# ScalarE's two steps of an attention round in the other order: exponentials of the present unit first, then the copy of the turned probabilities of three rounds back

## The reference

```python
def first_block(x, mem, ...):            # two layers
    h = rmsnorm(x, g_mix[l])
    dq, dk, dv, c_q, c_kv_kr, xq, gate_logits = jnp.split(h @ w_in[l], split_idx, axis=-1)
    y_diff = diff_attention(...) @ w_diff_o[l]      # 8 heads, two causal softmax maps each, keys of 64
    y_mla = latent_attention(...) @ w_mla_o[l]      # 8 heads, causal, keys of 96, values of 64
    y_mem = memory_cross_attention(...) @ w_cross_o[l]   # 4 heads of 128 over 256 memory rows
    gates = jax.nn.sigmoid(gate_logits + b_gate[l])
    x = x + (gates[0] * y_diff + gates[1] * y_mla + gates[2] * y_mem) @ w_out[l]
    x = x + jnp.square(jax.nn.relu(rmsnorm(x, g_mlp[l]) @ w_mlp1[l])) @ w_mlp2[l]

def hybrid_layer(x, ...):                # the second block, two layers
    p = split_cols(rmsnorm_2(x, norm_w) @ w_in)
    o_a = dsa_mixer(...)        # scores pick the keys, then a softmax over them
    o_b = nsa_mixer(...)        # three softmaxes: compressed, selected, window
    o_c, o_d = shortconv_mixer(...), pool_mixer(...)
    return x + jnp.concatenate([silu(gate) * o ...], axis=-1) @ w_out
```

## Time and profile before

| | us |
|---|---|
| median of 3 runs | 2902.8 (2900.97 to 2902.9) |
| the profiled execution | 2904.73 |
| its span | 2902.3 |
| TensorE matmuls busy | 2706.6 (93%) |
| TensorE weight loads busy | 2196.5 (76%) |
| GpSimd busy | 1868.5 (64%) |
| VectorE busy | 1076.0 (37%) |
| ScalarE busy | 758.2 (26%) |
| exponentials (L619), 352 | 172.5 busy |
| copies (L631), 176 | 116.6 busy |
| maxima (L605), 176 | 132.6 busy |
| transpositions (L546), 784 | 126.2 busy |

### The profile page before, as it was taken

The page is one execution under the profiler, slowest core; times in us unless marked ns, Lnnn a source line. Parts: engine busy times, 40 slices in busy tenths (PEclk is TensorE's granted clock), DMA queues, the critical chain, the costliest instruction groups (busy, mean ns, idle before and its releaser), DMA issues. The chain is left out here.

```text
span 2902.3 us, 38743 instructions
## 1 busy us (share of the span) xinstructions
PE 2706.6 (93%) x14204; PEld 2196.5 (76%) x14204; DVE 1076.0 (37%) x1936; ACT 758.2 (26%) x1469; POOL 1868.5 (64%) x1562
## 2 busy tenths in 40 slices
PE   6999999999999997999999999999998998989987
PEld 5788776877888886788777778888887875677755
DVE  4452555211210113344374310310112487526783
ACT  3331564100120201341465100120111214212251
POOL 5647223888898995748420888898886772366704
PEclk9999999999999998999999999999998997989988
DMA  4323101333233233323100233223234320142202
GB/s 122 102 56 83 33 8 27 87 94 92 91 98 95 94 98 77 113 66 82 46 8 9 82 92 98 88 95 98 95 97 84 89 79 28 33 86 76 80 1 73
DMA packets 159284, 214.77 MB, mean 74 GB/s; under 512 B 51696, under 2 KB 69360, under 8 KB 159088
## 3 DMA queue, kind: packets, MB, share of 16 engines
q1 hardware_dynamic: 120336, 207.27, 24.3%
q10 hardware_dynamic: 38752, 4.95, 1.4%
HBM read 210.06 MB, written 2.10 MB: 73 GB/s over the span
## 5 line engine op out<-in xcount | busy, mean ns | idle before, releaser
L293 POOL TENSOR_TENSOR weight_parts<-weight_ring,zero 128x512 fp32r<-128x512 f32 (+3 forms) x736 | 790.2, 1074 | 735.5 <-PE ps L376 368.4
L296 POOL TENSOR_TENSOR weight_parts<-weight_ring,weight_parts 128x512 fp32r<-128x512 f32 (+4 forms) x804 | 1062.6, 1322 | 129.4 <-ACT weight_parts L304 71.0
L378 PE MATMUL ps<-h_feature_major_high,weight_parts 128*128 128x512 f32 x2304 | 589.4, 395 | 17.9 <-POOL weight_parts L293 11.6
L378 PEld LDWEIGHTS ps<-h_feature_major_high,weight_parts 128*128 128x128 f32 x2304 | 431.3, 189 | 124.4 <-POOL weight_parts L293 19.4
L376 PE MATMUL ps<-weight_parts,h_feature_major_high 128*128 128x512 f32 (+3 forms) x1920 | 438.4, 368 | 18.7 <-POOL weight_parts L293 7.8
L376 PEld LDWEIGHTS ps<-weight_parts,h_feature_major_high 128*128 128x128 f32 x1920 | 341.7, 192 | 71.3 <-POOL weight_parts L293 8.2
L378 PE MATMUL ps<-h_feature_major_low,weight_parts 128*128 128x512 f32 x1152 | 311.5, 393 | 0.0
L376 PE MATMUL ps<-weight_parts,ut_high 128*128 128x512 f32 x1024 | 254.7, 390 | 0.0
L378 PEld LDWEIGHTS ps<-h_feature_major_low,weight_parts 128*128 128x128 f32 x1152 | 218.5, 190 | 46.5
L376 PE MATMUL ps<-weight_parts,h_feature_major_low 128*128 128x512 f32 (+3 forms) x960 | 231.6, 364 | 0.0
L524 PE MATMUL ps<-arena 64*128 64x512 f32 (+9 forms) x704 | 179.4, 509 | 49.6 <-ACT probs L619 29.4
(11 more groups left out here) (255 smaller groups left out, 2912.9 us busy)
## 6 DMA issues: line engine op xcount, KB each, us to landing
weight_ring<-in_w_in SPq DMA_DIRECT2D x272, 256.0 KB, 2.6
weight_ring<-in_w_mlp SPq DMA_DIRECT2D x256, 256.0 KB, 2.7
weight_ring<-in_w_out SPq DMA_DIRECT2D x64, 256.0 KB, 2.5
weight_ring<-in_w_mem_kv SPq DMA_DIRECT2D x32, 256.0 KB, 2.7
weight_ring<-in_w_diff_o SPq DMA_DIRECT2D x32, 256.0 KB, 2.7
weight_ring<-in_w_in SPq DMA_DIRECT2D x32, 170.0 KB, 2.4
weight_ring<-in_w_in SPq DMA_DIRECT2D x32, 168.0 KB, 2.2
weight_ring<-in_w_in SPq DMA_DIRECT2D x32, 163.0 KB, 2.2
```

The costliest lines, as they stand in the source:

```text
L293: self.nc.gpsimd.tensor_tensor(high, raw, self.m["zero"][:].broadcast_to([P, raw.shape[1]]), ALU.add).then_inc(self.s["slab_high"], 1)
L296: self.nc.gpsimd.tensor_tensor(low, raw, high.bitcast(F32), ALU.subtract).then_inc(self.s["slab_split"], 1)
L378: last = self.nc.tensor.matmul(banks[:, t, :], w[:, cut], h, **ends)
```

## The change

In the four calls of `A.steps` on ScalarE, `(0, A.exp)` comes ahead of `(3, A.copy)` in the list. TensorE, VectorE, GpSimd, SyncE and all waits keep their order and their form.

```diff
--- before.py
+++ after.py
@@ -1013,7 +1013,7 @@
             full(act, "dk1")
             square("dk1")
             empty("dk1", qk[:, :, 3 * W512:])
-            A.steps(0, U1, (3, A.copy), (0, A.exp), ahead=2)
+            A.steps(0, U1, (0, A.exp), (3, A.copy), ahead=2)
             roots(st_d[:, :, 24:32])
             empty("lat0", latq[:, :, 0:LATW // 2], width=LATW // 2)
             full(act, "lat1")
@@ -1042,7 +1042,7 @@
                     a.activation(km[:, t, 4 * k:4 * k + 4, 0:MNOPE], bank[:, :, 0:MNOPE], ACT.Copy, scale=st_lat[:, t, 1:2])
                     last = a.activation(vm[:, t, 4 * k:4 * k + 4, :], bank[:, :, MNOPE:], ACT.Copy, scale=st_lat[:, t, 1:2])
                 last.then_inc(emptied, 1)
-            A.steps(U1, U2, (3, A.copy), (0, A.exp), between={prep_rounds[-2]: lambda: roots(st_both)})
+            A.steps(U1, U2, (0, A.exp), (3, A.copy), between={prep_rounds[-2]: lambda: roots(st_both)})
             for k in range(2):
                 scaled(f"m_t{k}", [(qmt[0:MQK, 4 * k + h, :], h, MQK, SEQ, mqg[0:MQK]) for h in range(4)])
             for k in range(2):
@@ -1052,7 +1052,7 @@
                     act.wait_ge(s["weighted"], u + 1)
                     a.activation(ot[0][:, 8 + units[u]["pair"], :], ps[:, units[u]["bank"], :], ACT.Copy).then_inc(s["high_written"], 1)
 
-            A.steps(U2, U3, (3, A.copy), (0, A.exp), (4, round_high))
+            A.steps(U2, U3, (0, A.exp), (3, A.copy), (4, round_high))
             roots(st_o)
             for name in merge_order:
                 if name[0] == "o":
@@ -1583,7 +1583,7 @@
             empty("f1", [(fm[:, 8:10, :], L.banks("f1")[:, 0:2, :], ACT.Copy, 1.0), (fm[:, 10:12, :], L.banks("f1")[:, 2:4, :], ACT.Silu, 1.0)])
             empty("f2", [(fm[:, 12:14, :], L.banks("f2")[:, 0:2, :], ACT.Copy, 1.0), (fm[:, 14:16, :], L.banks("f2")[:, 2:4, :], ACT.Silu, 1.0)])
             empty("cmp_t", [(kcmpt, L.banks("cmp_t")[:, 0, 0:NCMP], ACT.Copy, 1.0)])
-            A.steps(0, U, (3, A.copy), (0, A.exp))
+            A.steps(0, U, (0, A.exp), (3, A.copy))
             L.square_right(act, 1, junk)
 
         @block.vector
```

## The result

The changed kernel takes 2983.28 us (median of 4 runs, 2979.08 to 2986.27) against 2901.89 us (4 runs, 2900.78 to 2902.9): a ratio of 1.0283, interval [1.027, 1.0296]. It is slower, as forecast; the forecast was 2969 us, the range 2925 to 3008. The profiled spans are 2902.3 and 2984.4 us, +82.1. In the experiments three executions that took 5368 to 9296 us (two of the kernel before, one of the kernel with the copy between the exponentials) are left out of every median, ratio and interval.

What follows compares the result with a forecast made beforehand. TensorE was taken to bound latent attention, VectorE's turn to decide in differential attention's start and the second block. First block 44, second 12, clock 10: +66 us on 2904.7, less 1.9, gives 2969; range 2925 to 3008.

Steps and rivals of the forecast that it cites:

- The mechanism: Attention rounds: TensorE's turning T(j+1) waits for ScalarE's copy C(j), now behind exponentials E(j+3); exponentials gain at most one copy, 0.38 to 0.81 us.
- The latent halves: Latent attention lap: turning of 512 keys to that of 384 takes 6.78 us (5.92 before), then 5.65 (4.63 before).
- The late differential halves: Differential attention's last twelve rounds, no woven work: 6.11 us (5.69 before) and 5.42 (4.82 before); +3 us a layer.
- Rounds 3 to 20 with woven work: Differential attention: the chain through VectorE's division and woven piece takes 7.87 us against 5.76; +11 us a layer, bounds 6 and 17.
- The second block: At 12 waits of scores for exponentials, a quarter of 1.6 to 2.7 us is lost; +6 us a layer, bounds 0 and 12.
- Latent attention: A lap of 10.55 us gets 1.9 longer over 3.3 laps, +6.3; with the last closing round +6.5 us a layer.
- Late differential rounds and cross attention: Last twelve differential rounds: three laps of +1.0, +3 us a layer; cross attention: six rounds, +1.5 us a layer.
- The clock: TensorE's waits bring seven more spells at the lower clock, about 1.4 us each over all layers: +10, bounds 0 and 24.
- (a): Rival, chance 0.04: wherever scores wait for exponentials, these come one copy earlier, 44 waits times 0.6 = 26 us, 2877.
- (b): Rival, chance 0.04: exponentials and copy both come soon enough, as TensorE has weighting and scores between; no change, 2903.
- (c): Rival, chance 0.14: VectorE's woven work hides the chain's loss; only stretches without it lose, 22 us, 2925.
- (d): Rival, chance 0.18: the attention passes see some 30 spells at 1.2 GHz instead of seven, +42 in place of +10, 3001.

## Why the prediction was right, and where its sizes were off

**The mechanism** held as it was put: C(j) behind E(j+3), T(j+1) behind C(j), a closed chain over two rounds. The latent halves were forecast at 6.78 and 5.65 us and measured at 6.84 and 5.72. The late differential halves are these turnings, of 512, 384 and 512 keys, after:

```profile
405.56 0.85 PEld L546 LDWEIGHTS ps<-ident,probs 128*128 128x128 f32 x8 [0.35 <-ACT probs L619]
...
411.73 0.64 PEld L546 LDWEIGHTS ps<-ident,probs 128*128 128x128 f32 x6
...
417.21 0.85 PEld L546 LDWEIGHTS ps<-ident,probs 128*128 128x128 f32 x8 [0.25 <-issue]
```

6.17 and 5.48 us, forecast 6.11 and 5.42. In the two latent ones the copy's signal took 0.11 and 0.12 us, where 0.05 was assumed. Shown by experiment: in cross attention the alternating banks take the link T(j+1) on C(j) away, and with it the whole loss ahead of the last maximum; the copy between the exponentials about halves the loss of the four passes together. Two of the signs that were to show it came out weaker than written: the copies' waits for turnings fell to 42.9 us and didn't vanish, and of the two late differential laps only the last took 11.65 us (11.5 was forecast), the one before it 12.6.

**Term by term.** The forecast without the clock was 56 us, and the passes gained 86.6. The difference of 30.6 lies in five places:
- *The closing rounds, 12.0 us.* The passes end later by 1.2 to 2.3 us behind the last maximum, 12.4 in all (last column of the first table); I had priced this for latent attention alone, at 0.2. The last copies stand behind the last exponentials too, and the rest of the pass follows them turning by turning. Some of this comes back right behind the passes, within the 4.5 us above.
- *Rounds 3 to 20 with woven work, 9.2 us.* The first five laps took 75.3 us against 59.7, +15.6 a layer where +11 was forecast. The chain was forecast at 7.87 and is 8.17: the copy's signal 0.12 for 0.05, and from the weighting's first load (354.41) to the division 1.20 us, where I had counted its eight weight loads (0.86) and not its last matmul's end; the rest came 0.11 shorter. The larger part is the weighting of the pairs: I took two thirds of nine pairs, and no loss in the pairs without a piece in their second round. The kernels without woven work lose in rounds without a piece as well (11.7 us a lap for 10.5), and the mean price of a piece rises from 0.6 to 1.25 us, the root's and the lower clock's share in it included. The root's two table loads were left out of the sum; "a table load doesn't move either" holds for their number, but a copy stood between root and second load before, and now comes behind the exponentials.
- *The second block, 5.4 us* in the rounds. A loss of 0.5 us at each of 12 places was taken; up to the last maximum it is 8.4 and 9.0 us, 0.7 a place. "VectorE has its own work for most of that" was the weak step: VectorE waits too. The maxima's waits for scores rose in this stretch (third layer) from 14.2 us in 8 to 21.1 in 12, and the turnings' wait for VectorE's scaling (L598), which I had not listed, is 10.3 us in 6 (in the whole program before 1.2 in 2):

```profile
ACT probs L619 <- DVE negmax L605: 32.3, 19, 4.0
DVE negmax L605 <- PE ps L529: 21.1, 12, 8.1
PE ps L546 <- ACT probs_key_major L631: 12.8, 10, 3.1
...
PEld ps L546 <- DVE probs L598: 10.3, 6, 3.3
```

- *Latent attention, 3.2 us.* 6.3 was forecast for the laps; layer 1 has 6.2, layer 2 9.6. The 3.4 between the two layers are the clock's (0.92 and 0.84; matmuls busy for 52.43 and 56.53 us), 3.0 of them in the first lap, where the clock is 0.69 and 0.50. In the pair without woven work, at 0.97 throughout, the loss up to the last maximum is 6.2 and 6.4 us: the forecast of the chain alone was right.
- *Late differential rounds and cross attention* were off by under 1 us together.

**The clock** was put at 10, and no run here shows that size. Separable are the 3.4 us of the second layer's latent pass. In differential attention the granted clock fell from 0.95 over 95.8 us to 0.91 over 116.1: as an estimate from these figures, the time at the lower level went from 10 to 21 us, and at half rate 11 more of it cost at most 5.5 us a layer. How much of that is on the path is open. The matmuls' busy time doesn't tell: it rose by 7.4 us there, and by 5.9 in the pair without woven work, where the clock is 0.96 and 0.95. In the second block it is 0.81 before and after. So the term may have been too large or about right. The price of a spell was taken from twelve weightings at 0.23 us each as against 0.11, which is the spacing of weight loads; twelve weightings at the full clock take 1.50 us (356.89, after), 0.13 each.

The total of 2969 came nearer to 2983 than its parts deserve: without the clock 56 us were forecast for what gained 86.6. Two things brought the totals closer: the 10 for the clock, a size that no run shows, and the 4.5 us that came back between the passes, which the forecast didn't hold. That is luck.

**The rivals.** (a) *Exponentials win*, 2877: no pass of the four got shorter. The scores' waits for exponentials did shrink, from 40.4 us in 44 to 10.1 in 20, as it says, and it was worth nothing. (b) *Nothing*, 2903: excluded by the four kernels with one pass each, whose intervals all lie above 1. (c) *VectorE hides it*, 2925: the reverse. Woven work makes the loss larger, 20.4 us a pass against 11.6 and 12.1. (d) *The clock falls for long*, 3001: its total is 18 us off, the forecast's 14, so the total doesn't part the two. The laps do: in latent attention they lose 2.0 us at a granted clock of 1.00, and 7.8 and 7.9 us a pass at 0.97 in the pair without woven work. *TensorE: Matmul & The Clock Gate* in the Trainium skill (section on HAM oscillation) has gaps in a loop, where they are long enough, put the engine back to half rate each time. The trace agrees for single gaps (eight transpositions in 1.57 us after 2.28 of idle, in 1.06 otherwise), but the 73 waits of the turnings are 1.1 us in the mean, and the clock over the program went only from 0.961 to 0.959.

Two points stay open: how much of differential attention's loss is the clock's, and why the rotations, in the first two laps, cost less than the squares (2.0 us for all four in the new order, spread).

## What to carry to other kernels

When two jobs share an in-order queue, don't ask which is needed more urgently, ask which is ready: the exponentials wait for a result that is still being made, the copy's input is there, and a ready job behind a waiting one delays everything behind itself. Look then for the single buffer that hands the delay on (here one set of turned banks): follow it once around until it closes, count every engine's queue on the way, the rounds that close a pass too, and treat woven-in work on such a queue as part of the chain, not as cover. A second buffer at that place can take most of the order's price away: in cross attention it left 0.7 us a pass of 2.0 to 2.8. In the other passes this was not tried; a unit of 512 keys fills both banks there.

## What the runs showed beside

- The first lap of a latent pass runs partly at the lower clock level, and for how long differs between layers and executions. After the change it takes 12.1 us at a granted clock of 0.69 in layer 1 (456.6 to 468.7 us) and 15.1 at 0.50, the lower level throughout, in layer 2 (1592.9 to 1608.0), for the same instructions. The old order took 54.1 us in one execution and 51.6 in another (the kernel with alternating banks in cross attention, whose latent pass is the old one), all of the difference in the first lap: 11.5 us at 0.61 and 8.9 at 0.89. The laps behind it are alike to 0.01 us there, at 1.00. So differences of under 3 us in such a pass say nothing by themselves.
- In the old order the 14 woven pieces cost 8.7 us a pass where they stand two rounds in three, and 3.5 where they stand every second round (81.0 and 75.8 against 72.3 without any). 2.2 of these 5.2 us are the first lap's, which holds three pieces in the one and two in the other; about 0.7 of the 2.2 vary from execution to execution.
